# Spare wide products ahead of the last sums and the spreading of two-scale norms, in a three-block transformer kernel on one core

## The reference

```
def rms_norm(x, g):
    xf = x.astype(jnp.float32)
    y = xf * lax.rsqrt(jnp.mean(xf * xf, axis=-1, keepdims=True) + EPS)
    return (y * g.astype(jnp.float32)).astype(x.dtype)
```

## Time and profile before

| what | value |
|---|---|
| median of three runs | 3772.44 us (3770.05 to 3775.42) |
| the profiled execution's own time | 3774.36 us |
| its span, from first to last instruction | 3772.6 us |
| TensorE matmul busy | 3620.7 us (96%) |
| weight loads of TensorE | 2893.9 us (77%) |
| DVE / ACT / POOL busy | 2062.0 us (55%) / 941.0 us (25%) / 1093.4 us (29%) |
| mean granted clock of TensorE | 0.987 |
| chain that ended last, by engine | PE 86%, DVE 9%, ACT 2%, DMA 2%, issue 1% |

### The profile page before, as it was taken

One profiled execution on the slowest core, in us unless ns is written; L12 is line 12 of the kernel. 1 busy time (PEld: TensorE's weight loads), 2 busy tenths in 40 slices (PEclk: granted clock), 3 DMA queues, 4 the chain that ended last, 5 costly groups with the idle time before them and its releaser, 6 DMA issues.

```text
span 3772.6 us, 46307 instructions
## 1 busy us (share of the span) xinstructions
PE 3620.7 (96%) x18230; PEld 2893.9 (77%) x18230; DVE 2062.0 (55%) x2828; ACT 941.0 (25%) x1672; POOL 1093.4 (29%) x1069
## 2 busy tenths in 40 slices
PE   7999999899999999999999999899999989999998
PEld 5677776688888888888887778577878868788776
DVE  5545546633333246699933443455526598663564
ACT  3434335300000004311101101231222113552132
POOL 2121221233333333233331132133233234014332
PEclk9999999999999999999999999999999999999999
DMA  2000100121212111122221121221283224422211
GB/s 97 23 29 18 34 29 18 56 67 61 68 60 72 56 61 56 41 94 89 79 77 62 34 78 56 78 74 61 79 161 95 81 80 126 144 94 79 72 52 66
DMA packets 139242, 260.21 MB, mean 69 GB/s; under 512 B 45632, under 2 KB 87616, under 8 KB 136000
## 3 DMA queue, kind: packets, MB, share of 16 engines
q1 hardware_dynamic: 72208, 156.26, 14.3%
q10 hardware_dynamic: 66864, 101.62, 7.8%
HBM read 209.35 MB, written 46.14 MB: 68 GB/s over the span
## 4 chain that ended last, share of the span: by engine, by line
PE 86%; DVE 9%; ACT 2%; DMA 2%; issue 1%; SPq 0%; POOL 0%; ACTq 0%; DVEq 0%; POOLq 0%
PE bank L653 24%; PE bank L656 23%; PE bank L657 23%; PE bank L908 2%; PE bank L1077 2%; PE bank L945 1%; PE bank L928 1%; PE bank L1066 1%; DVE fb L2208 1%; DMA raw<-in_wstream 1%; PE bank L793 1%; PE bank L1238 1%; PE bank L1221 1%; DVE ab L2211 1%; DVE h L2609 1%
## 5 line engine op out<-in xcount | busy, mean ns | idle before, releaser
L653 PE MATMUL bank<-xh,wh 128*128 128x512 f32 x3024 | 1191.6, 394 | 32.0 <-DVE xl L2075 12.3
L656 PE MATMUL bank<-xl,wh 128*128 128x512 f32 x3024 | 1181.6, 391 | 0.0
L657 PE MATMUL bank<-xh,wl 128*128 128x512 f32 x3024 | 1180.8, 390 | 0.0
L612 POOL CAST wh<-raw 128x512 fp32r<-128x512 f32 x528 | 344.3, 652 | 2471.3 <-PE bank L657 2327.2
L614 POOL TENSOR_TENSOR wl<-raw,wh 128x512 fp32r<-128x512 f32 x528 | 735.5, 1393 | 42.3
L653 PEld LDWEIGHTS bank<-xh,wh 128*128 128x128 f32 x3024 | 568.8, 188 | 173.1 <-issue 22.9
L657 PEld LDWEIGHTS bank<-xh,wl 128*128 128x128 f32 x3024 | 568.9, 188 | 121.8
L656 PEld LDWEIGHTS bank<-xl,wh 128*128 128x128 f32 x3024 | 569.2, 188 | 117.1 <-issue 0.5
L2372 DVE SCALAR_TENSOR_TENSOR bank<-apad,cols,bank 128x512 f32<-128x512 f32 x406 | 267.9, 752 | 0.0
L2113 DVE TENSOR_TENSOR h<-bank,h 128x512 f32<-128x512 f32 x240 | 165.6, 691 | 144.2 <-PE bank L657 143.5
L2241 DVE TENSOR_TENSOR gt<-sa,bank 128x512 f32<-128x512 f32 x44 | 30.3, 688 | 347.7 <-PE bank L657 347.7
(11 more groups left out here) (334 smaller groups left out, 4963.8 us busy)
## 6 DMA issues: line engine op xcount, KB each, us to landing
raw<-in_wstream SPq DMA_DIRECT2D x264, 512.0 KB, 3.5
spills<-spill ACTq DMA_DIRECT2D x38, 512.0 KB, 3.0
rawm<-in_mod_w ACTq DMA_DIRECT2D x12, 1024.0 KB, 4.8
gate_spill<-gates ACTq DMA_DIRECT2D x16, 512.0 KB, 2.6
tabs<-in_rope ACTq DMA_DIRECT2D x4, 2048.0 KB, 8.8
f<-spills SPq DMA_DIRECT2D x8, 1024.0 KB, 5.4
h<-in_x ACTq DMA_DIRECT2D x4, 1024.0 KB, 11.6
tabs<-gate_spill ACTq DMA_DIRECT2D x4, 1024.0 KB, 7.7
```

Of the source, the lines that this page charges most:

```text
L612: nc.gpsimd.tensor_copy(wh[:, slot, k], raw[:, slot, k]).then_inc(S("panel_high"), 1)
L653: mm = nc.tensor.matmul(o, lh, rh, start=start, stop=False, skip_group_check=shared)
L656: nc.tensor.matmul(o, lh, rl, start=False, stop=False, skip_group_check=shared)
L657: return nc.tensor.matmul(o, ll, rh, start=False, stop=stop, skip_group_check=shared)
```

## The change

A new helper issues a number of fp32r products of 128x128 by 512 columns, all of the same piece of `xh`, into bank 7. Nobody reads that bank at these places. The helper is called ahead of each of the last sums of `gate` (6 products, then 3), ahead of each of the last three sums of `pw` (3 each), and in `norm_end` ahead of the spreading of the two-scale norms (8). Since `gate` serves `gate3` too, `last_final` gets its 6 and 3. No wait is added, nothing else is moved, and no other engine's program changes. There are 17 spare products at `first_final`, 17 at `second_final` and 9 at `last_final`, 43 in all.

```
--- before.py
+++ after.py
@@ -830,8 +830,14 @@
                     if c % 4 == 3:
                         mm.then_inc(S(sem), 1)
 
+            def spare_products(many):
+
+                for _ in range(many):
+                    nc.tensor.matmul(banks[7][:, :], xh[:, 0, 0:P], xh[:, 0, 0:HALF], start=True, stop=True)
+
             def norm_end(name):
                 if NORMS_OF[name] == 2:
+                    spare_products(8)
                     norm_spread(name, 5, 2, "norm_spread")
                     norm_spread(name, 1, 5, "keep_spread")
 
@@ -1022,6 +1028,7 @@
                     if name == "gate1" and p in MOD_SUMS:
                         modulation(MOD_SUMS[p])
                 for k in range(KT - 2, KT):
+                    spare_products(6 if k == KT - 2 else 3)
                     norm_sum(norm, k)
                 norm_end(norm)
 
@@ -1135,6 +1142,7 @@
             if "pw" in run:
                 hidden_and_out("pw", yh, yl, "yl_ready", "second_final", split="conv_ln")
                 for k in range(KT - 3, KT):
+                    spare_products(3)
                     norm_sum("second_final", k)
                 norm_end("second_final")
             if "s5_u" in run:
```

## The result

The changed kernel takes 3778.85 us in the median of 17 runs (3775.57 to 3786.0). The kernel before took 3772.28 us beside it, in the median of 17 runs, one of which took 11594 us and is left out of the ratio. The ratio is 1.0017, with a 95% interval of 1.0010 to 1.0024: 6.6 us more, with 3.8 to 9.1 us inside the interval. The profiled execution is one of 3778.85 us, span 3777.1 us, mean granted clock 0.987, as before. TensorE's matmuls are busy for 3632.3 us, 11.6 more, in 43 more records.

A forecast was written before the change was run, and what follows sets the result against it. At the norms and the end, the chain of waits runs through the matmuls the change surrounds, partly at half clock. -0.5 (first_final) + 2.0 (second_final) + 0.65 (last_final) = +2.1 us, a median of 3774.5 us, range 3768 to 3781.

The forecast's parts named there:

- the case that was forecast: Both two-scale norms: clock lost late, or a mixture near it; +2.1 us in all, 3774.5 us; chance 0.45.
- rival (2): Both two-scale norms: clock lost early, the 8 at half clock delay the spreading; +7.9 us, 3780.3; chance 0.2 with rival (3).
- the 0.9 us by which a cheaper product would lower its sum: Second_final: at the skill page's 131 ns, nine spare products cost 1.2 us instead of 2.0, forecast 0.9 us lower.
- What can be won is tile 7's sum, 3.57 to 1.95 us: First_final: full clock saves 1.6 us in tile 7's sum, and 0.9 us in the spreading's first half.
- I take the late loss, -0.5 us: First_final: clock falls as the 8 products begin; -1.6 + 1.6 and half of the spreading's 0.9 us.
- the early one: First_final: clock lost before the second sum; +0.7 + 1.6 = +2.3 us, less 0 to 0.9 us in the spreading.
- The late loss: Second_final: only tile 7's sum is slow, +1.25 us; the 8 add 1.6, the spreading gives 0.9 back: +2.0 us.
- Nothing else in the program changes: Outside the three norms: weight stream, POOL's splits and DVE's work are released by the same instructions and move with them.
- Last_final: Program's end: 6 products hidden in 1.63 us of idle time, 3 between sums delay what follows; +0.65 us (0.5 to 0.7).
- Clock held at both: Rival (1), both two-scale norms: the clock stays up; -2.5 - 1.2 + 0.65 = -3.1 us, 3769.4; chance 0.25.
- Products without an effect on the clock: Rival (3): spare products neither keep nor restore the clock; upper end of rival (2), no spreading gain; chance 0.2 with it.
- Something else that shifts later falls of the clock: Rival (4), anywhere: something unseen, such as a shifted later low-clock stretch, moves time over 0.2% either way; chance 0.1.

The follow-up runs named there:

- sums only: Against the changed kernel, keeps only products ahead of the sums at the two two-scale norms (6 and 3; 3, 3 and 3): 3773.78 us, ratio 1.0006.
- first norm only: Against the changed kernel, spare products only at the first two-scale norm (6, 3 and 8): 3772.3 us, ratio 1.0001.
- second norm only: Against the changed kernel, spare products only at the second two-scale norm (3, 3, 3 and 8): 3778.2 us, ratio 1.0014.
- the 46 products: Against the changed kernel, 6 and 6 at the first norm's sums, 6 each at the second's, 8 ahead of both spreadings, none at the last: 3775.16 us, ratio 1.0004.
- the last two kernels: Against the changed kernel, only 6, 6, 6 at the second norm's sums: 3776.58 us, ratio 1.0006; only 6 and 3 at the first's: 3771.65 us, ratio 0.9997.

## Why the prediction held within its range, and was 4.4 us too low

The time lies in the range, and within 0.2% of before, as forecast. In this the width of the range helped: the time lies 4.4 us above the case that was forecast and 1.5 us below the early loss, which was rival (2). The forecast's +2.1 us was made of prices, +5.9 us (8 late at half clock 1.6 twice, nine products 2.0, the end 0.65), and of gains, -3.8 us. The runs let both be measured. Two slips of its working are small: the 0.1 us of the three products at `first_final` is left out of its -0.5 us, and the 0.9 us by which a cheaper product would lower its sum leaves out the three at the end (0.3 us).

**The prices were about right.** The prices below are from the durations of the forecast or of the kernel's own profile. Beside them stand the differences at equal clock, with 95% intervals:

| spare products | price from rows, us | at equal clock, us | by the mean clock, us |
|---|---|---|---|
| as changed | 0.1 to 0.7, 1.6, 2.0, 1.6, 0.65: 6.0 to 6.6 | +7.4 +-0.9 | -1.0 +-1.4 |
| the 8 at both | 1.6 + 1.6 = 3.2 | +3.1 +-1.1 | +2.5 +-2.3 |
| the 8 at the second | 1.6 | +1.7 +-1.1 | -0.6 +-1.2 |
| 8 narrow ones at both | 3.2 | +3.9 +-1.1 | +2.1 +-2.0 |
| 4 at both, 6 at the first | 2 x (2.05 - 1.83) = 0.4 | +0.3 +-1.1 | -0.1 +-1.7 |
| 24 at both | 6.4 + 5.2 = 11.6 | +12.8 +-1.6 | +0.7 +-3.9 |
| sums only | 0.1 to 0.7, 2.0: 2.1 to 2.7 | +2.9 +-1.1 | -1.0 +-1.8 |
| first norm only | 0.1 to 0.7, 1.6: 1.7 to 2.3 | +1.4 +-1.1 | -1.3 +-2.5 |
| second norm only | 2.0 + 1.6 = 3.6 | +3.4 +-1.1 | +1.1 +-1.6 |
| 6, 6, 6 and 8 at the second; 6, 6, 8 at the first | 4.1, 0.3, 0.8 to 2.0, 1.6: 6.8 to 8.0 | +6.6 +-1.1 | -4.4 +-2.1 |
| 6, 6, 6 at the second | 18 x 0.227 = 4.1 | +4.4 +-1.1 | -1.3 +-2.2 |
| 6, 3 at the first | 0.1 to 0.7 | -0.6 +-1.1 | -0.3 +-1.5 |

Each price meets its measured interval, three of them with a part of their own span only (the changed kernel, the 46 products, the first norm's 6 and 3). The parts added (8 at both, sums only, and the end: 3.1 + 2.9 + 0.65 = 6.7 us) agree with the whole (7.4 +-0.9). That this line divides truly is a reading of runs whose clock nobody set; what speaks for it is that it was used ahead of the last two kernels and met their prices within 0.3 and 0.7 us.

A price here is the later start alone, not the loss that the rows show at the norm, since the line books a shorter time at the lower clock under the clock. With the 8 at both norms the rows hold 1.5 us, and the 40 us around `first_final` have 0.83 in place of 0.79, 3.2 us less of the lower clock, or 1.1 us by the line: 2.6 us together, within the +3.1 +-1.1. The other way round, 3.2 us more at half clock lower a run's mean by 0.0004 of themselves, or 1.1 us by the line. So the division is not sharper than about 1 us. With a constant for each chip beside those for the kernels no difference of the experiments moves by more than 0.5 us.

**The gains were the step that failed.** "What can be won is tile 7's sum, 3.57 to 1.95 us", the shorter spreading, and the second norm's sums were booked at full size. This step took a shorter time at half clock, counted in one execution, for a gain of every run; the overhang was priced rightly. By 0.35 us for a microsecond at the lower clock, -3.8 us would need 11 us less of that clock in a run, a mean higher by 0.0014. The changed kernel has 0.0004 (+-0.0005): -1.0 us. Three things show why:
- *First_final.* "I take the late loss, -0.5 us": the profile shows the early one and +1.8 us, as the forecast had priced that case (+2.3 less up to 0.9). Another execution of the same instructions showed the late one. It is not one case, but a mixture.
- *Second_final.* The late loss came as forecast, and so did its local size (+1.7 us against +2.0). But the gain was counted from one execution of before, in which the three sums took 7.93 us. Where nothing stands ahead of them, six of nine profiles have them at 5.7 to 6.1 us (as the 6.08 us above), and three, that of before among them, at 7.9 to 8.1: in these six there was no 2.3 us to win.
- *Behind the norms.* "Nothing else in the program changes" holds for the instructions, not for the clock: it fell longer at 2770 to 2830 and 3030 to 3135, and not at all at 3440 to 3475 and 3615 to 3655.

*Last_final* was right: 0.70 us against 0.65. So was the wait of ACT that hides the six products (0.27 us of it are left), and so was the size of the 8 at half clock (3.3 to 3.8 us against 3.43).

**The rivals.** Clock held at both (3769.4): it fell. Early loss at both (+7.9 us): nearest in size, and its mechanism, the 8 at half clock ahead of the spreading, is the largest price; but in the profile only one of the two losses was early. Products without an effect on the clock: the kernel of 46 products, whose mean clock rose by 0.0017, speaks against it; in the changed kernel the effect is not told from nothing. Something else that shifts later falls of the clock: there in the pair of profiles above, 6 to 7 us in single stretches, but without a sign that the runs could tell.

The Trainium skill's page TensorE: Matmul & The Clock Gate (What's actually happening) says that the count of slow products at a kernel's start differs from run to run, and advises against fitting to one count. No run here counts them; the 100 runs of before show a mean clock from 0.984 to 0.989, and 3781.1 to 3766.7 us along it. The forecast quoted the first half of it and then fitted its gains to one execution all the same.

What stays open: whether delays at the norms lower the mean clock by themselves (the 8 at both, wide or narrow, show 0.0010 and 0.0008 less, at the edge of their intervals of 0.0009 and 0.0008).

## What to carry to other kernels

Filler work put into a wait has to fit the wait at the clock at which it will run there, not at the clock that it is meant to keep: here 1.81 us of products at full clock were 3.4 at half clock, and of the nine places with 8 of them in these profiles eight met half clock. Book such a price in full, and a gain from the clock only as far as the mean granted clock of many runs rises, since a single profile shows one of several cases. When times scatter with a quantity that is recorded for each run, compare at equal values of it: here that halved the scatter and made prices of 2 us readable.

## What the runs showed of the hardware

- A run's time follows its mean granted clock, which differs between executions of one kernel from 0.984 to 0.989: 2.6 us for each 0.001, half of all the scatter.
- 16 records of 128x128 fp32 products shortened the spreading behind them (5.87 to 3.83 us) as much as 8 products of 512 columns did (3.73 us): the granted clock of that spreading was 0.97, where it was 0.50 for the first 4.2 us before.
- Six products (1.36 us) ahead of each sum of `second_final` stood beside a clock of 1.00 through all three sums, in both kernels that had them; with three (0.68 us) the third sum was at 0.50 in all three profiles that had them. The price of the six ate what the clock gave back: +4.4 and -1.3 us alone, +6.6 and -4.4 us in the kernel of 46 products.
